# The hybrid decoder layer: the value product one paired step later, with one run of projections per step and one gate tile projected early

## The reference

```
proj = h @ w_in                       # q, k, v, gates z and g of all branches
ya = softmax(q k^T / 8 + c[t] - c[s]) v      # branch a, 8 heads, forgetting
yb = attention over the 256 best keys by an indexer   # branch b, 8 heads
yc = dilated windows (128,1), (512,4), (2048,16)      # branch c, 12 heads
ya, yb, yc = y * silu(z)
merged = sigmoid(ga) * (ya @ w_a) + sigmoid(gb) * (yb @ w_b) + sigmoid(gc) * (yc @ w_c)
out = rmsnorm(x + merged @ w_o)
```

## Time and profile before

| | us |
|---|---|
| median of 3 runs | 1592.64 (1592.2 to 1597.14) |
| profiled execution, whole time | 1591.12 |
| its span, first to last instruction | 1589.3 |
| PE busy | 1472.4 (93%) |
| PE weight loads busy | 1158.2 (73%) |
| DVE busy | 775.8 (49%) |
| ACT busy | 701.2 (44%) |

### The profile page before, as it was taken

How to read it: one execution, slowest core, us unless ns; L and a number is a source line. 1 busy time by engine, 2 the same in 40 slices (tenths; PEclk the granted TensorE clock), 3 DMA queues, 4 the chain that set the end, 5 groups by cost and what they waited for, 6 DMA issues and landing times.

```text
span 1589.3 us, 21557 instructions
## 1 busy us (share of the span) xinstructions
PE 1472.4 (93%) x8082; PEld 1158.2 (73%) x8082; DVE 775.8 (49%) x1667; ACT 701.2 (44%) x1530; POOL 67.1 (4%) x142
## 2 busy tenths in 40 slices
PE   4888889999999999999999997999999999999898
PEld 3666566666666778887777775778888878888786
DVE  5455845444455897552333334554544455323534
ACT  6345665556666452112454556444444442211312
POOL 1103300000000000000000000100000000000000
PEclk9988999999999999999999999999999999999999
DMA  5114511111111112222101000311232212222332
GB/s 167 34 54 113 139 27 34 27 34 27 34 34 34 34 40 63 73 73 84 34 21 27 21 21 1 121 40 52 70 97 69 77 51 67 66 73 81 126 100 106
DMA packets 111512, 97.17 MB, mean 61 GB/s; under 512 B 10672, under 2 KB 98096, under 8 KB 111152
## 3 DMA queue, kind: packets, MB, share of 16 engines
q1 hardware_dynamic: 100816, 58.54, 13.8%
q0 software_dynamic: 10592, 37.23, 7.5%
HBM read 73.21 MB, written 18.35 MB: 58 GB/s over the span
## 4 chain that ended last, share of the span: by engine, by line
PE 75%; DVE 6%; ACT 4%; issue 3%; ACTq 0%; DVEq 0%; DMA 0%; POOL 0%; POOLq 0%
PE bank L766 19%; PE bank L768 18%; PE bank L767 18%; PE bank L934 5%; PE bank L961 3%; PE slot L921 2%; PE slot L911 2%; DVE idle_out L1371 2%; PE slot L897 1%; PE slot L766 1%; PE slot L896 1%; PE slot L768 1%; PE slot L767 1%; ACT pta L1228 1%; ACT pa L1215 1%
## 5 line engine op out<-in xcount | busy, mean ns | idle before, releaser
L766 PE MATMUL bank<-hs,w_hl 128*128 128x512 f32 x1152 | 466.8, 405 | 10.4 <-DVE tm L1631 5.5
L767 PE MATMUL bank<-hs,w_hl 128*128 128x512 f32 x1152 | 452.5, 393 | 0.0
L768 PE MATMUL bank<-hs,w_hl 128*128 128x512 f32 x1152 | 452.5, 393 | 0.0
L766 PEld LDWEIGHTS bank<-hs,w_hl 128*128 128x128 f32 x1152 | 218.4, 190 | 64.3 <-issue 17.2
L768 PEld LDWEIGHTS bank<-hs,w_hl 128*128 128x128 f32 x1152 | 217.8, 189 | 48.3
L767 PEld LDWEIGHTS bank<-hs,w_hl 128*128 128x128 f32 x1152 | 218.4, 190 | 42.0 <-issue 0.8
L1344 DVE TENSOR_TENSOR w_hl<-w_raw,w_hl 128x512 fp32r<-128x512 f32 (+1 forms) x176 | 118.7, 678 | 260.2 <-ACT w_hl L1052 256.9
L1052 ACT ACTIVATE w_hl<-w_raw 128x512 fp32r<-128x512 f32 (+1 forms) x176 | 108.9, 620 | 180.1 <-PE bank L768 177.3
L1371 DVE TENSOR_SCALAR_CACHE_REDUCE idle_out<-score,state 128x512 uint8<-128x512 f32 (+4 forms) x140 | 115.3, 824 | 5.0
L1546 DVE TENSOR_TENSOR ptb<-bank,ptb 128x512 fp32r<-128x512 f32 (+2 forms) x96 | 50.5, 554 | 137.7 <-ACT ptb L1225 137.6
L1243 ACT ACTIVATE yb<-bank 64x128 f32<-64x128 f32 x64 | 17.2, 269 | 148.4 <-PE bank L768 148.4
(11 more groups left out here) (304 smaller groups left out, 2402.7 us busy)
## 6 DMA issues: line engine op xcount, KB each, us to landing
w_raw<-in_w_in_dram SPq DMA_DIRECT2D x142, 256.0 KB, 2.8
merged_scratch<-ms POOLq DMA_DIRECT2D x16, 512.0 KB, 3.3
ms<-merged_scratch POOLq DMA_DIRECT2D x16, 512.0 KB, 4.0
xn<-in_x_dram SPq DMA_DIRECT2D x8, 512.0 KB, 6.6
iq_st<-iq_hl POOLq DMA_DIRECT2D x32, 128.0 KB, 3.2
qb<-qb_scratch POOLq DMA_DIRECT2D x8, 512.0 KB, 4.2
w_raw<-in_w_o_dram SPq DMA_DIRECT2D x16, 256.0 KB, 4.0
qb_scratch<-bq_high POOLq DMA_DIRECT2D x8, 256.0 KB, 3.5
```

The lines of the kernel that those rows point to most:

```text
L766: pe.matmul(out_, wh, mh, start=start, stop=False)
L767: pe.matmul(out_, wh, ml, start=False, stop=False)
L768: return pe.matmul(out_, wl, mh, start=False, stop=stop)
```

## The change

1. `pair_run` lasts one step more. `pv` of step s-2 stands between the logits of s and the turn of s-1, and the two pumps become one of twice the rate (1.6) at the end of the step.
2. `v_turn` of a tile stands one step later, behind the first logits and their pieces.
3. `c_bcast` are written one by one in the last five steps of the tile before (for the first tile all four at its start). negc becomes four buffers, and the broadcast reads one column of `sel` with stride zero, so selA goes.
4. Of the gate z of branch a, the first tile is projected in the last tile of a: four pieces, one each in the steps b = 4 to 7 (kind `ea`, read by `z_early`, which multiplies y in place). Its share factor, the product and the split follow in `z_shared`, in phase b.
5. Branch b's filling is pumped at 0.89 pieces a step; a's merge has 60 pieces where it had 64.
6. The picking steps `bound` and `count` are cut: their six counts are now two steps of three each.

```diff
@@ -51,6 +51,7 @@
+EARLY = 1
@@ -92,6 +93,18 @@
+    def split(br, c):
+        for t in range(2):
+            step("z_split", c=c, th=t, zn=count["z"] - 2 + t, hs=nxt("hs"), br=br)
+
+    def shared(br, c):
+
+        for th in range(2):
+            share = ring()
+            step("share", br=br, c=c, th=th, u=share)
+            step("z_shared", br=br, c=c, th=th, zn=nxt("z"), share=share)
+        split(br, c)
+
@@ -99,14 +112,15 @@
         def read(th):
-            name = kind[0] if kind[0] in "zgw" and len(kind) == 2 else kind
+            name = kind[0] if kind[0] in "zgw" else kind
             if name == "z":
                 step("share", br=kw["br"], c=c, th=th, u=share)
-                step("z", c=c, u=u, th=th, zn=nxt("z"), share=share, **kw)
+                step("z", c=c, u=u, th=th, zn=nxt("z"), zt=nxt("zt"), share=share, **kw)
                 if th:
-                    for t in range(2):
-                        step("z_split", c=c, th=t, zn=count["z"] - 2 + t, hs=nxt("hs"), br=kw["br"])
+                    split(kw["br"], c)
+            elif kind == "ea":
+                step("z_early", c=c, u=u, th=th, zt=nxt("zt"))
             else:
@@ -181,7 +195,7 @@
-    picking = [("bit", n) for n in range(32)] + [("bound", 0), ("count", 0)]
+    picking = [("bit", n) for n in range(32)] + [("bound", 0), ("above", 0), ("above", 1), ("count", 0), ("equal", 0), ("equal", 1)]
     picking += [(kind, i) for i in range(2, TB) for kind in ("ties", "mask")]
@@ -204,7 +218,10 @@
                 plan.append(("logits", x))
-            if s:
+            if s >= 2:
+                units[s - 2]["pv"] = ring()
+                plan.append(("pv", units[s - 2]))
+            if 1 <= s <= n:
                 x = units[s - 1]
@@ -216,12 +233,11 @@
                     pick()
-            pump(rate)
-            flush_later()
-            if s:
-                x["pv"] = ring()
-                plan.append(("pv", x))
-            pump(rate)
+            x = units[min(s, n - 1)]
+            if x["br"] == "a" and x["ch"] == NCH["a"] - 1:
+                pump(1 if x["b"] >= 4 else 0)
+            else:
+                pump(2 * rate)
             flush_later()
@@ -229,21 +245,23 @@
         for ch in range(NCH[br]):
+            def next_fill(ch=ch):
+                flush()
+                fill.extend(qkv(br, ch + 1) if ch + 1 < NCH[br] else after())
+
             def v_turns(ch=ch):
-                flush()
                 for half in range(2):
                     step("v_turn", br=br, ch=ch, half=half, use=tiles["V" + br, ch, half])
-                fill.extend(qkv(br, ch + 1) if ch + 1 < NCH[br] else after())
             at = len(units)
-            before.setdefault(at, []).append(v_turns)
+            before.setdefault(at, []).append(next_fill)
+            before.setdefault(at + 1, []).append(v_turns)
             if br == "a":
-                def bcast(ch=ch):
-                    for th in range(2):
-                        for h in (2 * ch, 2 * ch + 1):
-                            tiles["negc", h, th] = ring()
-                            step("c_bcast", h=h, th=th, u=tiles["negc", h, th])
-                before.setdefault(at, []).append(bcast)
+                for i in range(4):
+                    def bcast(h=2 * ch + i % 2, th=i // 2):
+                        tiles["negc", h, th] = ring()
+                        step("c_bcast", h=h, th=th, u=tiles["negc", h, th])
+                    before.setdefault(at - 5 + i if ch else 0, []).append(bcast)
             for b in range(TB):
@@ -260,8 +278,12 @@
         n = NCH[br]
-        for c in range(n):
-            yield from tile_pieces("z" + br, c, "h", br=br)
+        early = EARLY if br == "a" else 0
+        for c in range(early, n):
+            for piece, _ in enumerate(tile_pieces("z" + br, c, "h", br=br)):
+                for done in {0: (0,)}.get(piece, ()) if early and c == early else ():
+                    shared(br, done)
+                yield
         yield from tile_pieces("g" + br, 0, "h", br=br)
@@ -331,13 +353,13 @@
     step("phase", name="a")
-    attend("a", lambda: [])
+    attend("a", lambda: [tile_pieces("ea", c, "h") for c in range(EARLY)])
     step("phase", name="b")
     softmax_run([dict(br="b", ch=h // 2, hh=h % 2, b=b, W=(b + 1) * P, h=h)
-                 for h in range(B_HEADS) for b in range(TB)], {}, 0.95)
+                 for h in range(B_HEADS) for b in range(TB)], {}, 0.89)
     flush()
@@ -434,7 +456,7 @@
-        negc, selA = at(44, "negc", [P, 2, T]), at(52, "selA", [ROWS, A_HEADS, P], F32R)
+        negc = [at(k, f"negc{k}", [P, T]) for k in (44, 48, 52, 64)]
@@ -444,7 +466,7 @@
-        tm = at(48, "tm", [P, 4, HALF])
+        tm, tm_early = at(48, "tm", [P, 4, HALF]), at(72, "tm_early", [P, 2, HALF])
@@ -540,7 +562,7 @@
-                src = [(0, cols(w_in[0], COL[kind] + (c if kind != "ckv" else 0) * P))]
+                src = [(0, cols(w_in[0], COL["za" if kind == "ea" else kind] + (c if kind != "ckv" else 0) * P))]
@@ -872,10 +894,10 @@
-                    pe.wait_ge(sel_ready, 3)
+                    pe.wait_ge(sel_ready, 1)
-                    pe.matmul(bank[u[0]][:], selA[:, a["h"], :], rowsT[:, th * HALF:(th + 1) * HALF],
+                    pe.matmul(bank[u[0]][:], sel[:, a["h"], 0:1].to_broadcast([ROWS, P]), rowsT[:, th * HALF:(th + 1) * HALF],
@@ -1184,11 +1206,11 @@
-                    if a["h"] >= 2:
-                        act.wait_ge(logit_ready, last_logit["a", a["h"] // 2 - 1] + 1)
+                    if a["h"] >= 4:
+                        act.wait_ge(logit_ready, last_logit["a", a["h"] // 2 - 2] + 1)
-                    A(negc[:, a["h"] % 2, th * HALF:(th + 1) * HALF], bank[u[0]][:], ACTF.Copy,
+                    A(negc[a["h"] % 4][:, th * HALF:(th + 1) * HALF], bank[u[0]][:], ACTF.Copy,
@@ -1282,6 +1304,13 @@
+                elif kind == "z_early":
+                    th = a["th"]
+                    full(act, a["u"][th])
+                    full(act, tiles["Va", NCH["a"] - 1, 1])
+                    if a["c"]:
+                        act.wait_ge(early_done, 2 * (a["c"] - 1) + th + 1)
+                    A(tm_early[:, th, :], bank[th][:], ACTF.Tanh, scale=0.5).then_inc(z_tanh, 1)
@@ -1411,8 +1440,6 @@
-                    if a["name"] == "a":
-                        spread(selA, A_HEADS)
@@ -1567,8 +1594,12 @@
                     then(v.copy_predicated(carry, keep, bits))
+                elif kind in ("above", "equal"):
                     for j in range(PICKS):
-                        then(count(j, ALU.is_gt))
+                        if j % 2 == a["n"]:
+                            then(count(j, ALU.is_gt))
+                    if kind == "equal" and a["n"]:
+                        then(v.tensor_scalar(need, val, -1.0, float(TOPK), ALU.mult, ALU.add))
                 elif kind == "count":
@@ -1577,9 +1608,6 @@
-                    for j in range(PICKS):
-                        then(count(j, ALU.is_gt))
-                    then(v.tensor_scalar(need, val, -1.0, float(TOPK), ALU.mult, ALU.add))
@@ -1635,6 +1663,23 @@
                     v.tensor_tensor(tm[:, 2 * th + 1, :], z, Y[br][:, c, ts], ALU.mult).then_inc(z_mul, 1)
+                elif kind == "z_early":
+                    c, th = a["c"], a["th"]
+                    y, z = Y["a"][:, c, th * HALF:(th + 1) * HALF], tm_early[:, th, :]
+                    dve.wait_ge(z_tanh, a["zt"] + 1)
+                    v.scalar_tensor_tensor(z, z, 1.0, bank[th][:], ALU.add, ALU.mult).then_inc(bank_free[th], 1)
+                    freed(dve, a["u"][th])
+                    freed(dve, last_pv["a", c])
+                    v.tensor_tensor(y, y, z, ALU.mult).then_inc(early_done, 1)
+                elif kind == "z_shared":
+                    br, c, th, sh = a["br"], a["c"], a["th"], a["share"]
+                    full(dve, sh)
+                    if c:
+                        dve.wait_ge(low_ready, split_of[br, c - 1, th] + 1)
+                    v.tensor_tensor(tm[:, 2 * th + 1, :], Y[br][:, c, th * HALF:(th + 1) * HALF], bank[sh[0]][:],
+                                    ALU.mult).then_inc(z_mul, 1)
+                    dve.wait_ge(z_mul, a["zn"] + 1)
+                    dve.sem_inc(bank_free[sh[0]], 1)
                 elif kind == "z_split":
```

More of the change, by code:

```diff
@@ L69, in build_plan @@
     plan, uses, blocks = [], [0] * 4, []
-    count = {"ring": 0, "tp": 0, "hs": 0, "S": 0, "L": 0, "unit": 0, "z": 0, "bp": 0, "qk": 0}
+    count = {"ring": 0, "tp": 0, "hs": 0, "S": 0, "L": 0, "unit": 0, "z": 0, "zt": 0, "bp": 0, "qk": 0}
     tiles, unit_of_tp, units_seen = {}, [], []
@@ L197, in pair_run @@
         defer[0] = True
-        for s in range(n + 1):
+        for s in range(n + 2):
             for f in before.get(s, []):
@@ L488, in hybrid_layer_kernel @@
         share_diff, share_exp, share_ready = sem("share_diff"), sem("share_exp"), sem("share_ready")
```

(4 more changed lines are left out.)

1 line of the change is left out of this document (removed).

## The result

The changed kernel takes **1544.95 us** (median, 1544.7 to 1546.6), beside 1594.38 us of the kernel before in the same rounds. The ratio is 0.969, 95% interval 0.967 to 0.971: 49 us faster, where 27 were forecast, and outside the range of 1556 to 1577. Its profiled execution took 1545.0 us with a span of 1543.1, which is 46 us under the profiled one of before.

What follows compares the result with a forecast made beforehand. TensorE (PE), busy 93%, was taken as the bound, so only its waits could go: 6.9 + 4.9 + 7.0 + 2.1 + 4.7 + 3.8 + 2 - 2.5 = 28.9, kept at 27, forecasting 1565 us, range 1556 to 1577.

Steps and rivals of the forecast that it cites:

- The overhang of a wait: All PE waits: each costs about 0.1 us beyond its idle row; some 30 waits give 3 us, 2 taken.
- Part 1: Branches c and a: value product one step later removes its waits, 6.9 us in c and 4.9 in a.
- Part 2: Branch c: turning v one step later removes its waits for ACT's copy, 7.0 us, lower end 5.
- Part 3: Starts of c and a: first turn's wait shortens by 1.1 us, a's earlier logits give 1.0; together 2.1.
- Part 4: Branch a's tile changes: broadcasts one by one, not four in a row, gain 4.7 us; stride-zero operand priced at zero.
- Part 5: Last tile of a: gains 3.8 us of its 9.2 idle; 10.9 us of projections move there at no net cost.
- Part 6: Branch b: more steps and products without a piece cost 2.5 us, between 0 and 9.
- Part 7: c's merge: picking the top keys in smaller steps is the same DVE work; 0, plus or minus 1 us.
- The clock rival: Starts of c and a: both clock falls vanish, 2 x 3 us more come back, 1559 us; 12%.
- The ring: Branches c and a: turns wait 0.25 us more for a shared bank, 72 steps cost 18 us, 1583; 7%.
- Exponentials late at every turn: Turn of s-1 in all 80 steps of c and a: at 0.5 us late each, 40 us lost, 1606; 3%.
- The 1.9 us kept back: Whole sum: held back from the 28.9 us gain for open losses of the value product, v turn and broadcasts, leaving 27.

Runs made afterwards that it cites:

- the second profile: The changed kernel, with no further edit, profiled a second time: c took 284.7 us and its first turn waited 1.7 us.
- the last experiment: The changed kernel with the lag of the value product everywhere but in the last tile of branch a: 1547.04 us, ratio 0.972.

## Why the prediction was wrong, point by point

The direction, the list of waits and most of their prices were right. The size was half. By stages of the profiles, 46.2 us: 26.4 in c, 19.2 in a and b, 0.5 ahead of c, less 1.4 in c's merge, and 1.4 at the end.

**The missing term: two pumps became one.** The part on what the change does names it, and the prediction prices nothing for it: "nothing in this change shortens a matmul". It was taken as a matter of order. 24 steps of c and 12 of a lose a run (72 to 48, and 36 to 24 in a's first three tiles). At 0.22 to 0.27 each that is some 5.9 us in c and about 3 in a, by the same price. The experiment on the second run in c shows 9 us of busy time and 13 in all, since waits return as well. The rows to find it stood in the trace of before: a matmul follows another of its run after 0.227 us, but the whole steps with two pieces took longer than their parts.

**The overhang of a wait** was sized 0.1, from one tile change; the steps of c show 0.25. At some 30 waits that is 7 or 8 us and not 2. This is the second mis-sized term.

**Part 1, the value product: the saving right, the cause wrong.** 6.9 were forecast for c, and 6.9 of the 8.0 went; the last product's 1.1 stayed, as forecast. But the single run removes them, as the kernel before with one run shows. The lag alone is worth at most 3 us. The worry about late exponentials had no place in the steps with pieces, and its price of 0 was right there.

**Part 2, v turned later:** 7.0 forecast, gone, with no wait in its place; but only beside the single run. Alone it lost 3.3 to the products.

**Part 3, the starts.** In a the logits start 3.5 us behind the merge's last matmul (5.7 before): 2.2, less the turn of v that comes later, as forecast. In c the first turn waited 0.3 and not 2.2, yet it came 8.2 us behind the first logits where it came 7.4: PE ran its pieces at half clock meanwhile. The wait went into the matmuls; in the second profile, at a granted clock of 0.72 and not 0.50, it waited 1.7 and came at the same place (8.2). With the turn of v (1.2) now in between, the start gained some 0.4 of the 1.1 forecast.

**Part 4, the broadcasts:** 4.7 forecast, 4.0 measured. The operand read with stride zero costs nothing. The weight loads of the broadcasts after, then before (ns: least, median, most):

```profile
L900 PEld LDWEIGHTS bank<-rowsT,sel x16: 185/188/188, 720.0 to 888.9; 128*128 128x128 f32 x16
```

```profile
L878 PEld LDWEIGHTS bank<-rowsT,selA x16: 186/186/288, 748.1 to 950.8; 128*128 128x128 f32 x16
```

**Part 5, the early tile.** The walk-through was good in the one wait that mattered: 0.6, 0.7 and 2.1 were forecast for the waits for exponentials, and PE in the last tile shows

```profile
917.89 0.66 PE L956 MATMUL bank<-ident,pa 128*128 128x128 f32 x4 [0.30 <-ACT pa L1237]
...
920.36 0.87 PE L956 MATMUL bank<-ident,pa 128*128 128x128 f32 x6 [0.33 <-ACT pa L1237]
...
923.31 1.25 PE L943 MATMUL slot<-ka,qa 64*128 64x512 f32 x12 [2.08 <-ACT pa L1237]
```

From its first logits the tile took 50.4 us with 10.9 of moved work and the turn of v (1.2) inside, 40.8 before: 2.5 gained for a forecast of 3.8. What the walk left out is the clock behind the third wait (busy time by stretch); where it did not fall, with two runs in c, the same tile took 48.8 us, and 1.6 more make the gain 4.1:

```profile
921.00:924.00 3.00, 0.92 (x9) 0.60 (x8) 0.56 (x2) 2.21 (x6) 0.00 (x0) 1.00 0.01 3
924.00:927.00 3.00, 3.00 (x27) 2.55 (x24) 2.27 (x6) 0.28 (x1) 0.00 (x0) 0.59 0.00 0
```

**Part 6, branch b thinner:** 2.5 forecast, 0.3 measured (10.9 us left b, which became 10.6 shorter). The thin steps waited as forecast, 6.2 us in 8 times for 4.1 in 5 before. But the waits of the shares went from 2.0 us to 1.1 and those of the turns from 1.3 to 0.6, so in all the waits grew by under 1 us. Before (995 to 1312), then after:

```profile
PE bank L766 <- DVE ptb L1546: 4.1, 5, 1.5
```

```profile
PE bank L788 <- DVE ptb L1573: 6.2, 8, 1.5
PE bank L1022 <- DVE ptb L1573: 1.1, 1, 1.1
```

**Part 7, the picks:** 0 plus or minus 1 forecast; c's merge is 1.2 shorter with the finer steps, and the medians can't tell.

**The rivals.** The clock rival's 1559 came closest of all the times, but mostly by luck: it said that the clock would not fall at either start. It fell at both. At the start of a it fell for about half as long as before (0.57 over the eight us from 748 before, 0.79 after), which by the clock alone gives back some 1.7 us of the rival's 3 for that start. In one profile, that of the last experiment, it did not fall there at all. After, as the earlier trace rows, at the start of c and of a:

```profile
194.00:200.00 6.00, 5.62 (x16) 4.36 (x17) 3.52 (x7) 2.62 (x5) 2.07 (x7) 0.51 0.44 126
...
719.00:727.00 8.00, 6.53 (x23) 4.35 (x22) 2.74 (x9) 3.60 (x9) 0.53 (x1) 0.79 0.29 99
```

The ring: the turns' bank waits in a stayed, 3.9 us for 4.0, and 0 in c. Exponentials late at every turn: not with pieces in the step, but it is what the last tile does without them, and what a second run brings back at the starts of tiles. The 1.9 us kept back for losses of parts 1, 2 and 4 had no cause.

**The account for c:** 15.0 us of waits forecast and 16.9 found (15.5 in the second profile); 1.7 of overhang, and 4.0; nothing for the runs, and 5.9. For a and b: 11.9 forecast without overhang, 19.2 found. Of the 7.3, some 3 are runs, 2.2 branch b, and the rest waits' overhang; the clock gave 1.7 at the start of a and took 1.6 in its last tile. That split was worked out and not measured by itself.

## What to carry to other kernels

Count how often PE changes between kinds of work, not only how long it waits: compare whole steps, start to start, with one piece more or fewer, and what remains is the price of a switch, which hides in busy time. When several edits are made together, try the plainest alone; here moving filler in front of the dependent instruction did what the pipelining was credited with. And filler is a budget: a lag without filler makes a longer chain, and filler taken from the next stage is missed there once its cover is thin.

## What the runs showed of the hardware

- A switch out of a run of 128x512 matmuls and back costs PE 0.22 to 0.27 us at full clock, with no idle row. The same matmuls of c were busy 282.65 us with one run a step and 291.65 with two, some 2 of these 9 being the overhang of more waits.
- A wait of PE costs some 0.25 us more than its idle row: 0.94 for a row of 0.69, 0.86 for 0.55, 0.74 for 0.47, by whole steps.
- One wait of 2.08 us among short matmuls, with PE busy 0.92 of 3 us, was followed by a granted clock of 0.59 in the next 3 us, that is, a fall to 1.2 GHz for most of them. The same wait of 2.08 us at the same place, with PE busy 0.88 of 3 us, was followed by a granted clock of 1.00 in the kernel with two runs in c. In c's merge of before PE idled 3.0 us and kept 2.4 GHz. So neither the length of one wait nor the work around it tells. Such a fall cost the last tile of a 1.6 us, as much as the edits under test, and has to be looked for before a stage's gain is put down to an edit. Without the early tile the same happened more than once: the granted clock of 912 to 957 is 0.89 there, 0.96 with it.
- In the two kernels that were profiled twice, c, c's merge, a and b repeated within 0.2 us, start to start, while the times of one kernel's executions differ by 2 to 7 us. Between kernels c's merge took 238.0 to 241.5 us though no edit but that of the picks is in it. For an edit worth a few us the stage that it touches says more than the median.
